# Latent attention: the keys of two heads projected in one block, and the rows of odd heads turned round

## The reference, cut to what matters

```python
B_HEADS, B_NOPE, B_ROPE, B_V, B_Q_RANK, B_KV_RANK = 16, 64, 32, 64, 256, 128
cq, ckv, kr, g = jnp.split(h @ w_in, splits, axis=-1)
q = (rmsnorm(cq, q_norm_g) @ w_uq).reshape(bsz, S, B_HEADS, B_NOPE + B_ROPE)
qn, qr = q[..., :B_NOPE], apply_rope(q[..., B_NOPE:], cos, sin)
kv = (rmsnorm(ckv, kv_norm_g) @ w_ukv).reshape(bsz, S, B_HEADS, B_NOPE + B_V)
kn, v = kv[..., :B_NOPE], kv[..., B_NOPE:]
kr = apply_rope(kr, cos, sin)
...
s = (jnp.einsum('bqhd,bkhd->bhqk', qn_b, kn_all)
     + jnp.einsum('bqhr,bkr->bhqk', qr_b, kr_all)).astype(jnp.float32) * scale
p = jax.nn.softmax(s, axis=-1).astype(dt)
return jnp.einsum('bhqk,bkhd->bqhd', p, v_all)
```

## Time and profile before

| | us |
|---|---|
| median of 3 executions | 1574.75 (1574.63 to 1576.04) |
| span of the profiled execution | 1578.2 |
| values and heads 0 and 1, 1281.0 to 1299.5 | 18.5 |
| the attention with its `up` parts, from 1299.5 | about 193 |
| quads without `up` parts | 11.54 each |
| output projection and the end, from about 1520 | 58 |

### The profile page before, as it was taken

One profiled execution on the slowest core, in us unless ns is written; L12 is line 12 of the kernel. 1 busy time (PEld: TensorE's weight loads), 2 busy tenths in 40 slices (PEclk: granted clock), 3 DMA queues, 4 the chain that ended last, 5 costly groups with the idle time before them and its releaser, 6 DMA issues.

```text
span 1578.2 us, 21757 instructions
## 1 busy us (share of the span) xinstructions
PE 1515.5 (96%) x8728; PEld 1239.1 (79%) x8728; DVE 784.6 (50%) x1494; ACT 649.7 (41%) x1057; POOL 538.7 (34%) x472
## 2 busy tenths in 40 slices
PE   6999999999979999999999999999998989999997
PEld 6898988888768878888788987766787866666676
DVE  2868177283576315441465314777325445444423
ACT  6333333332532332123530325777424325555652
POOL 3433234332344364446332333333431330111231
PEclk9999999999989999999999999999998999999999
DMA  6533323234112145433212110210111220000011
GB/s 215 179 103 126 115 76 112 91 103 128 54 54 59 60 164 173 149 118 107 94 60 74 54 63 0 75 31 11 39 57 41 67 54 11 11 21 27 32 49 54
DMA packets 129395, 122.71 MB, mean 78 GB/s; under 512 B 11428, under 2 KB 125232, under 8 KB 129296
## 3 DMA queue, kind: packets, MB, share of 16 engines
q1 hardware_dynamic: 129182, 121.30, 24.3%
q10 hardware_dynamic: 114, 0.03, 0.0%
HBM read 116.87 MB, written 2.10 MB: 75 GB/s over the span
## 4 chain that ended last, share of the span: by engine, by line
PE 84%; DVE 11%; ACT 2%; issue 1%; SPq 0%; DMA 0%; POOL 0%; DVEq 0%; ACTq 0%
PE ps L2102 10%; PE ps L2104 10%; PE ps L2103 10%; PE ps L2577 4%; PE ps L2598 3%; PE ps L2163 3%; PE ps L2425 3%; PE ps L2587 3%; PE ps L2416 3%; PE ps L2323 3%; PE ps L2322 2%; PE ps L2324 2%; PE ps L2191 2%; PE ps L2578 2%; DVE q_two L1424 2%; PE ps L2094 2%
## 5 line engine op out<-in xcount | busy, mean ns | idle before, releaser
L1189 POOL TENSOR_TENSOR w_lo<-raw,w_hi 128x512 fp32r<-128x512 f32 x320 | 425.4, 1361 | 708.5 <-ACT w_hi L703 650.1
L2102 PE MATMUL ps<-h_hi,w_hi 128*128 128x512 f32 x632 | 254.9, 403 | 8.3 <-DVE u_g L1623 4.3
L2104 PE MATMUL ps<-h_hi,w_lo 128*128 128x512 f32 x632 | 248.8, 394 | 0.0
L2103 PE MATMUL ps<-h_lo,w_hi 128*128 128x512 f32 x632 | 248.8, 394 | 0.0
L703 ACT ACTIVATE w_hi<-raw 128x2048 fp32r<-128x2048 f32 (+1 forms) x77 | 145.5, 1890 | 126.5 <-PE ps L2104 52.0
L2102 PEld LDWEIGHTS ps<-h_hi,w_hi 128*128 128x128 f32 x632 | 120.7, 191 | 37.4 <-issue 11.5
L2104 PEld LDWEIGHTS ps<-h_hi,w_lo 128*128 128x128 f32 x632 | 120.2, 190 | 26.1
L2103 PEld LDWEIGHTS ps<-h_lo,w_hi 128*128 128x128 f32 x632 | 120.6, 191 | 23.9 <-issue 0.2
L1991 DVE CUSTOM_DVE_ANT_0 prob_b<-ps,no_mask 128x768 f32<-128x768 f32 x64 | 61.1, 954 | 72.7 <-PE ps L2578 72.7
L1131 ACT ACTIVATE pT_b<-ps 128x512 f32<-128x512 f32 x96 | 52.1, 594 | 71.3 <-PE ps L2587 71.3
L2094 PE MATMUL ps<-w_hi,h_hi 128*128 128x256 f32 x256 | 73.6, 287 | 0.0
(11 more groups left out here) (452 smaller groups left out, 3417.2 us busy)
## 6 DMA issues: line engine op xcount, KB each, us to landing
raw<-in_w_in_dram SPq DMA_DIRECT2D x32, 1024.0 KB
raw<-in_ada_w_dram SPq DMA_DIRECT2D x12, 1024.0 KB
raw<-in_a_w_in_dram SPq DMA_DIRECT2D x10, 1024.0 KB
raw<-in_w_in_dram SPq DMA_DIRECT2D x16, 512.0 KB
ada_strip<-in_ada_w_dram SPq DMA_DIRECT2D x7, 1024.0 KB, 6.4
ada_half<-in_ada_w_dram SPq DMA_DIRECT2D x10, 512.0 KB, 3.6
raw<-in_b_w_in_dram SPq DMA_DIRECT2D x5, 1024.0 KB
raw<-in_w_proj_a_dram SPq DMA_DIRECT2D x4, 1024.0 KB
```

What stands on the lines that cost most here:

```text
L1189: last = nc.gpsimd.tensor_tensor(w_lo[:, ph.w(s), p], raw[:, s % 2, p], w_hi[:, ph.w(s), p].bitcast(F32), ALU.subtract)
L2102: mm(ps[:, j, :], wh[:, k, c], xh[:, k, :], start=(k == 0), stop=False)
L2103: mm(ps[:, j, :], wh[:, k, c], xl[:, k, :], start=False, stop=False)
L2104: last = mm(ps[:, j, :], wl[:, k, c], xh[:, k, :], start=False, stop=(k == KT - 1))
```

## The change

TensorE's `up(m, part)` now makes a pair of heads in four parts: part 0 the keys of both heads for the latent tokens in one block of 64 + 64 weight columns (three products of 512), part 1 the same for the context tokens (three of 256), part 2 the queries of the even head and part 3 those of the odd head (six of 512 each). The even head's keys come out in rows 0 to 63, the odd head's in rows 64 to 127. So an odd head has its own part of the keys in rows 64 to 127 and the rotated rows in 0 to 63; its query weights are loaded in that order, and its queries are multiplied by a new table `turn_o`, which holds cosines and sines in the order of the odd head. The table lies in the second slot of `raw`. VectorE empties parts 0 and 1 by two copies each, one for either head, before it frees the bank.

A pair takes its four parts in two iterations, at their first and second place; the third place is empty. The loads of a pair are seven DMAs with rows of 256 and 128 bytes (before: five, with rows of 1024, 384 and 128 bytes), the splits have 640 columns and not 768, and SyncE's queue has the load of `turn_o` behind those of pair 1, and a wait for the last emptied part (`s_upe` at 32) ahead of the second strip of `b_w_o`.

```diff
@@ SyncE, loads of pair m
-                for h in range(2):
-                    sp.dma_start(dst[:, :, h, 0:B_QK], src[:, :, h, :]).then_inc(s_rup[m % 2], 16)
-                    sp.dma_start(dst[:, :, h, B_QK:P], src[:, :, h, B_NOPE:B_QK]).then_inc(s_rup[m % 2], 16)
-                sp.dma_start(raw[:, m % 2, UP + 4 * P:UP + 6 * P], t["b_w_ukv_1_2"][:, 2 * m * P:(2 * m + 2) * P]).then_inc(s_rup[m % 2], 16)
-            plain(b_out, t["b_w_o_1_2"], 0)
+                keys_of = t["b_w_ukv_1_2"][:, 2 * m * P:(2 * m + 2) * P].rearrange("p (h a c) -> p h a c", h=2, a=2)[:, :, 0, :]
+                sp.dma_start(raw[:, m % 2, UP + 4 * P:UP + 5 * P].rearrange("p (h c) -> p h c", h=2), keys_of).then_inc(s_rup[m % 2], 16)
+                for h, n0 in ((0, 0), (1, 2 * B_ROPE)):
+                    sp.dma_start(dst[:, :, h, n0:n0 + B_NOPE], src[:, :, h, 0:B_NOPE]).then_inc(s_rup[m % 2], 16)
+                    for r0 in (B_NOPE - n0, B_QK - n0):
+                        sp.dma_start(dst[:, :, h, r0:r0 + B_ROPE], src[:, :, h, B_NOPE:B_QK]).then_inc(s_rup[m % 2], 16)
+                if m == 1:
+                    sp.wait_ge(s_lo, b_v.k(0, 1) + 1)
+                    sp.dma_start(turn_o[:, :], t["turn_o"]).then_inc(s_taba, 16)
+            load(b_out, 0, 0, [(k_of(raw, 0), cols_of(t["b_w_o_1_2"], 0))])
+            sp.wait_ge(s_upe, 2 * B_HEADS)
+            for n in range(1, 4):
+                load(b_out, n // 2, n % 2, [(k_of(raw, n % 2), cols_of(t["b_w_o_1_2"], n * STRIP))])
@@ VectorE
-            def up(h, part):
-                dve.wait_ge(s_up, 3 * h + part + 1)
-                if part == 0:
-                    last = v.tensor_tensor(q_b[h % 4][:, :], ps[:, 7, :], cos_b[:, :], ALU.mult)
-                elif part == 1:
-                    last = v.tensor_copy(k_b[h % 4][0:B_NOPE, C:ALL], ps[0:B_NOPE, 7, :])
-                else:
-                    last = v.tensor_copy(k_b[h % 4][0:B_NOPE, 0:C], ps[0:B_NOPE, 7, 0:C])
+            def up(m, part):
+                dve.wait_ge(s_up, 4 * m + part + 1)
+                for h in (2 * m, 2 * m + 1):
+                    r = nope_rows(h)
+                    if part == 0:
+                        last = v.tensor_copy(k_b[h % 4][r, C:ALL], ps[r, 7, :])
+                    elif part == 1:
+                        last = v.tensor_copy(k_b[h % 4][r, 0:C], ps[r, 7, 0:C])
+                    elif part == 2 + h % 2:
+                        if h == 1:
+                            dve.wait_ge(s_taba, 16 * 4)
+                        last = v.tensor_tensor(q_b[h % 4][:, :], ps[:, 7, :], (turn_o if h % 2 else cos_b)[:, :], ALU.mult)
                 last.then_inc(s_upe, 1)
...
-                if nv >= B_KEYS:
-                    up((nv - B_KEYS) // 3, (nv - B_KEYS) % 3)
+                if B_KEYS <= nv < B_KEYS + 4:
+                    up(0, nv - B_KEYS)
...
-                    if u and x < B_QUADS - 2:
-                        up(x + 2, u - 1)
+                    if u % 2 and x < B_QUADS - 2:
+                        up(x // 2 + 1, 2 * (x % 2) + u // 2)
@@ TensorE
-                    c = slice(UP + (4 + j) * P, UP + (5 + j) * P)
-                    tk = slice(C, ALL) if part == 1 else slice(0, C)
-                    o = ps[:, 7, 0:S if part == 1 else C]
+                    c = slice(UP + 4 * P, UP + 5 * P)
+                    tk = slice(0, C) if part else slice(C, ALL)
+                    o = ps[:, 7, 0:C if part else S]
...
                 for b in range(0, B_KEYS, 2):
-                    if x < B_QUADS - 2:
-                        up(x + 2, b // 2)
+                    if x < B_QUADS - 2 and b < 4:
+                        up(x // 2 + 1, 2 * (x % 2) + b // 2)
```

More of the change, by code:

```diff
@@ L236, in block_kernel @@
         sin_b = at("sin_b", [P, S], F32, r_ya + 26 * KB)
+        turn_o = at("turn_o", [P, S], F32, r_raw + 8 * KB)
         vb = at("vb", [P, NC + NT, D], F32, r_yb)
@@ L540, in key_parts, with nope_rows, rope_rows @@
             return parts
+        def nope_rows(h):
+            return slice(0, B_NOPE) if h % 2 == 0 else slice(B_NOPE, P)
+        def rope_rows(h):
+            return nope_rows(h + 1)
         def k_of(a, slot, n=STRIP):
@@ L1114, in up_hi @@
             def up_hi(m):
-                act.wait_ge(s_rup[m % 2], 80 * (m // 2 + 1))
+                act.wait_ge(s_rup[m % 2], 16 * 7 * (m // 2 + 1))
                 if m >= 2:
-                    act.wait_ge(s_up, 6 * (m - 1))
-                c = slice(UP, UP + 6 * P)
+                    act.wait_ge(s_up, 4 * (m - 1))
+                c = slice(UP, UP + 5 * P)
                 nc.scalar.activation(w_hi[:, m % 2, c], raw[:, m % 2, c], ACT.Copy).then_inc(s_hi, 1)
@@ L1158, in _ @@
                     n = x - (B_QUADS - 3)
-                    hi(b_out, 0, n, (s_up, 6 * (7 + n)))
+                    hi(b_out, 0, n, (s_up, 4 * (7 + n)))
             b_split(KT - 1)
@@ L1317, in up_lo @@
             def up_lo(m):
-                lo(b_up, m // 2, m % 2, slice(UP, UP + 6 * P))
+                lo(b_up, m // 2, m % 2, slice(UP, UP + 5 * P))
             def b_spread(x):
@@ L1963, in _ @@
             for n in range(2):
-                link(v.tensor_copy(k_b[n][both, :], keys[both, :]))
+                link(v.tensor_copy(k_b[n][rope_rows(n), :], keys[both, :]))
             link(v.memset(no_mask[:, :], 0.0))
-            def up(h, part):
-                dve.wait_ge(s_up, 3 * h + part + 1)
-                if part == 0:
-                    last = v.tensor_tensor(q_b[h % 4][:, :], ps[:, 7, :], cos_b[:, :], ALU.mult)
-                elif part == 1:
-                    last = v.tensor_copy(k_b[h % 4][0:B_NOPE, C:ALL], ps[0:B_NOPE, 7, :])
-                else:
-                    last = v.tensor_copy(k_b[h % 4][0:B_NOPE, 0:C], ps[0:B_NOPE, 7, 0:C])
+            def up(m, part):
[10 more added lines that the diff above has]
+                        last = v.tensor_tensor(q_b[h % 4][:, :], ps[:, 7, :], (turn_o if h % 2 else cos_b)[:, :], ALU.mult)
                 last.then_inc(s_upe, 1)
@@ L1980, in _ @@
                     v.tensor_copy(vb[:, nv % B_KEYS, nv // B_KEYS * S:(nv // B_KEYS + 1) * S], ps[:, 0, :]).then_inc(s_vb, 1)
-                if nv >= B_KEYS:
-                    up((nv - B_KEYS) // 3, (nv - B_KEYS) % 3)
-            link(v.tensor_copy(k_b[3][both, :], keys[both, :]))
+                if B_KEYS <= nv < B_KEYS + 4:
+                    up(0, nv - B_KEYS)
+            link(v.tensor_copy(k_b[3][rope_rows(3), :], keys[both, :]))
             def b_max(x, u):
@@ L2527, in v_cols, with up @@
                 return w[:, s, 0:D].rearrange("p (h a c) -> p h a c", a=2, c=B_V)[:, :, 1, :]
-            def up(h, part):
-                s, j = h // 2 % 2, h % 2
+            def up(m, part):
+                s, j = m % 2, part % 2
                 if part == 0:
-                    pe.wait_ge(s_lo, b_up.k0 + h // 2 + 1)
-                if 3 * h + part:
-                    pe.wait_ge(s_upe, 3 * h + part)
-                if part == 0:
+                    pe.wait_ge(s_lo, b_up.k0 + m + 1)
+                if 4 * m + part:
+                    pe.wait_ge(s_upe, 4 * m + part)
+                if part >= 2:
                     for k in range(2):
@@ L2570, in b_scores @@
                 if i == u == 0:
-                    pe.wait_ge(s_upe, 6 * (j + 1))
+                    pe.wait_ge(s_upe, 4 * (j + 1))
                 if n >= 2:
@@ L2683, in tables @@
     cos_b, sin_b = rotary(B_ROPE, 1, B_NOPE)
+    crossed = sin_b[B_NOPE:].reshape(2, 2, B_ROPE // 4, S)[:, ::-1].reshape(B_ROPE, S)
+    turn_o = np.concatenate([cos_b[B_NOPE:], crossed, cos_b[:B_NOPE]])
     mask_a = np.zeros((P, C + 3 * BLK), np.float32)
@@ L2688, in tables @@
     return {"ident": np.eye(P, dtype=np.float32), "masks": masks, "cos_a": cos_a, "sin_a": sin_a,
-            "cos_b": cos_b, "sin_b": sin_b, "mask_a": mask_a}
+            "cos_b": cos_b, "sin_b": sin_b, "turn_o": turn_o, "mask_a": mask_a}
 OUT_SHAPE = (1, S, D)
```

## The result

The changed kernel takes 1565.65 us (median of four executions, 1565.08 to 1566.82); the kernel before, four executions with it, 1574.69. The ratio is 0.994, with a 95% interval from 0.9927 to 0.9953: 7.4 to 11.5 us less. The forecast was 1564.9, with a range of 1563.2 to 1569.4. A second measurement, six executions of the changed kernel and eleven of the kernel before, gave 0.9938 (0.9923 to 0.9953).

What follows compares the result with a forecast made beforehand. The prediction took TensorE's queue to bound the attention, and hand-overs between TensorE and VectorE the stretch ahead. Savings of 6.9 + 2.1 + 0.9 = 9.9 us took 1574.75 to 1564.9 us, range 1563.2 to 1569.4.

Steps and rivals of the forecast that it cites:

- The bound: In the attention TensorE's queue is the time; a product taken out is worth its start-to-start distance.
- Pairs 2 to 7: Iterations 2 to 13: even ones 12.59 us, odd ones 14.30; 1.15 us saved a pair, 6.9 us in all.
- The walk of the even iteration: Even iterations, followed from the first product of `up`: no new wait, 1.3 us to spare at the bank.
- The tightest hand-over: Even iteration, ScalarE's copies of blocks 2 and 3 ahead of blocks 4 and 5: in time, 0.6 us to spare.
- Pair 1: Iterations 0 and 1: 2.4 us saved in the first, 0.3 given back in the second, net 2.1 us.
- Pair 0: Beside the value groups ahead of the attention: first scores at 1298.7 in place of 1299.57, 0.9 us saved.
- The edits at nothing: SyncE's extra DMAs and wait, the `turn_o` load, and reshuffled copies and multiplications: costed at nothing.
- A: Pairs 0 and 1: hand-overs shift without shortening, only products go; 8.05 us saved, 1566.7 us; chance 0.15.
- B: Every iteration: a new wait from late ScalarE or key copies; 5.6 us lost, 1570.5 us; chance 0.11.
- C: Iteration 0 and pair 0: TensorE's clock falls to 1.2 GHz for one even iteration; slower, 1577.5 us; chance 0.04.
- The sum: Whole kernel: 6.9 + 2.1 + 0.9 = 9.9 us less, 1564.9 us.

Runs made afterwards that it cites:

- four banks: Changed kernel with the four parts of pair 0 in banks of their own and no TensorE wait between them; 1565.91 us, ratio 0.9934 to the kernel before.
- strip 1 late: Changed kernel with SyncE issuing the second strip of `b_w_o` only after ScalarE's exponential of tile 2 of quad 14; 1570.58 us, one execution.
- key products twice: Changed kernel with the three products of each key part made twice into the same bank; 1574.57 us, ratio 0.9994 to the kernel before.

## Why the prediction was right, point by point

**The bound.** TensorE's queue is the time in the attention. TensorE is busy for every us of the changed kernel's iterations, and putting the 48 products back puts back their price to 0.02 us (8.42 against 8.40 expected).

**Pairs 2 to 7**, predicted 6.9 us: 28.08 - (12.60 + 14.32) = 1.16 a pair, 7.0 in all. The prices of rows 3 to 5 held to 0.02 us an iteration, with the seam in its place.

**The walk of the even iteration.** No wait came up, and copies that hold the bank 1.2 us longer still fit in. The tightest hand-over, blocks 4 and 5, held too. The weights of the next pair are ready earlier than before: GpSimd ends at 1344.61 in the changed kernel, first use at 1345.55, so 0.94 us to spare against 0.56.

```profile
1342.92 1.69 POOL L1206 TENSOR_TENSOR w_lo<-raw,w_hi 128x512 fp32r<-128x512 f32 x2 [9.91 <-ACT w_hi L1136]
...
1345.55 0.48 PE L2566 MATMUL ps<-ckv_hi,w_hi 128*128 128x512 f32 x1
```

**Pair 1**, predicted 2.1 us: first scores to block 0 in 10.26 us, as walked (10.3), 2.41 less than before, and 0.3 given back in iteration 1. One step of the walk was not so: it had TensorE wait 0.2 us for VectorE's reading of tile 2 ahead of quad 1's scores. That reading ended at 1301.64 and the scores started at 1301.81, right behind the context keys, which took 0.54 us from their start to the scores and not 0.4. That the one nearly makes up for the other is luck, though a small piece of it.

**Pair 0**, predicted 0.9 us, measured 0.51: this is the term that was mis-sized. Here is part 2 of the changed kernel, which starts behind a wait:

```profile
1289.31 0.50 PE L2559 MATMUL ps<-cq_hi,w_hi 128*128 128x512 f32 x1 [0.26 <-DVE k_b L1991]
1289.65 0.40 PE L2560 MATMUL ps<-cq_lo,w_hi 128*128 128x512 f32 x1
1289.89 0.40 PE L2561 MATMUL ps<-cq_hi,w_lo 128*128 128x512 f32 x1
```

the same part in the kernel with four banks, where it doesn't wait:

```profile
1291.31 0.39 PE L2561 MATMUL ps<-cq_hi,w_hi 128*128 128x512 f32 x1
1291.54 0.39 PE L2562 MATMUL ps<-cq_lo,w_hi 128*128 128x512 f32 x1
```

and the second product of part 1 of head 0 in the kernel before, whose first is in rows 8:

```profile
1291.60 0.39 PE L2546 MATMUL ps<-ckv_lo,w_hi 128*128 128x512 f32 x1
```

In the changed kernel part 1 starts 3.11 us behind the start of group 6, as walked. But behind a wait the second product follows the first by 0.34 us (1289.31 to 1289.65) and not by 0.23 as without one, and part 1, of 256 columns, has 0.22 in place of 0.12. So each of the three parts behind a wait costs some 0.11 us more. I had multiplied the distance in a running stream, although the kernel before has the same restart: 1291.26 to 1291.60. The walk came to 10.53 us from group 6 to the first scores (1288.17 to 1298.7) and 10.89 were measured; three restarts make 0.33 of the missing 0.36. The small rest is not followed up: the walk rounds up by 0.1 us on its way (1295.0 + 1.38 is put at 1296.45), and leaves out some 0.05 us each time the bank goes back to TensorE (copy done at 1289.26, next product at 1289.31).

**The edits at nothing.** SyncE's wait and `turn_o` cost nothing, with more cover than I had counted: the table was issued at 1281.30 and first used at 1293.46, and its load takes 2.7 us. **The rivals.** A (waits stay, 8.05 us saved) is out by iteration 0 and the stage, though not by the medians alone, whose interval reaches down to 7.4 us; B (new waits) is out by the window without a gap; C (the clock) did not happen there: 1.00 from 1277 to 1515 us, also in the kernels that have more waits.

**The sum.** 7.0 + 2.1 + 0.5 = 9.6 us in the stage, 9.04 between the medians. The difference of half a us is inside the spread of both medians, which comes from ahead of the stage.

## What to carry to other kernels

When one engine's queue is gapless in a stage, price an edit by start-to-start distances, and check that no hand-over loses its cover by walking one iteration of each kind. Where the engine waits at hand-overs, count each restart as well, and ask first whether a free bank takes the hand-over away: here four idle banks were worth 2.0 us in a stretch of 11. Compare the stage and not the span, as soon as something ahead of it varies from one execution to the next.

## What the runs showed of the hardware that was not expected

TensorE's second product behind a wait starts 0.31 to 0.34 us after the first where a running stream has 0.23 (both of 512 columns, clock 1.00). And TensorE, whose part ahead of the stage is the same in all these kernels, came to it at 1277.0 to 1278.2 us in some executions and at 1281.4 to 1281.9 in others, whatever the kernel. The extra time at the lower clock lies between 400 and 500 us in two of the late ones (0.91 in the kernel before and with strip 1 late, against 0.95 to 0.97 in the others) and between 700 and 800 in the other two (0.95 with key products twice and with four banks, against 0.97 to 0.98). Why one execution has more of it than another stays open.
